# Twelve products of constants at each border between layers, in a whole network written as one kernel

## What is computed

```
x = x + nsa_mixer(rms_norm(x, ...), ...)                 # sparse attention, 16 heads
x = x + swiglu(rms_norm(x, ffn_norm[0]), ...)            # FFN 1
shared_k, shared_v = shared_mla_kv(x, ...)
x = x + mla_mixer(rms_norm(x, ...), shared_k, shared_v, ...)
x = x + swiglu(rms_norm(x, ffn_norm[1]), ...)            # FFN 2
# second block, two layers of
x = x + 0.5 * rmsnorm(ffn(rmsnorm(x, g_pre)), g_post)    # FFN 3, FFN 5
x = x + rmsnorm(mixer(rmsnorm(x, mix_pre)), mix_post)    # convolution, then differential attention
x = x + 0.5 * rmsnorm(ffn(rmsnorm(x, g_pre)), g_post)    # FFN 4, FFN 6
```

## Time and profile before

| | |
|---|---|
| median of 3 runs | 1904.44 us (1902.37 to 1904.89) |
| span of the profiled execution, first to last instruction | 1903.4 us |
| TensorE busy in it | 1733.7 us (91%) |
| VectorE, ScalarE, GpSimd busy | 1227.8, 815.2, 38.3 us |
| mean granted clock of TensorE | 0.959 of full speed |
| DMA | 285.93 MB, mean 150 GB/s |

### The profile page before, as it was taken

The page is one execution under the profiler, slowest core; times in us unless marked ns, Lnnn a source line. Parts: engine busy times, 40 slices in busy tenths (PEclk is TensorE's granted clock), DMA queues, the critical chain, the costliest instruction groups (busy, mean ns, idle before and its releaser), DMA issues.

```text
span 1903.4 us, 29255 instructions
## 1 busy us (share of the span) xinstructions
PE 1733.7 (91%) x11365; PEld 1593.9 (84%) x11365; DVE 1227.8 (65%) x1737; ACT 815.2 (43%) x1199; POOL 38.3 (2%) x23
## 2 busy tenths in 40 slices
PE   7879999997697999999989869999999989689997
PEld 7857799986577999899988769998899979579997
DVE  4778566666666666666668856665665654856665
ACT  4556443335444333533443054333443344743333
POOL 0000000000004000000000000000000000000000
PEclk9979999998799999999989989999899989889999
DMA  7510344453223455455444034545345445035444
GB/s 266 207 45 1 101 166 179 185 192 117 88 70 124 180 190 190 145 195 189 175 155 155 1 120 168 188 175 197 143 172 194 183 159 166 1 100 199 176 187 165
DMA packets 53291, 285.93 MB, mean 150 GB/s; under 512 B 5872, under 2 KB 6128, under 8 KB 30704
## 3 DMA queue, kind: packets, MB, share of 16 engines
q1 hardware_dynamic: 52224, 281.46, 41.0%
q0 software_dynamic: 1008, 3.67, 0.6%
HBM read 284.05 MB, written 1.05 MB: 150 GB/s over the span
## 4 chain that ended last, share of the span: by engine, by line
PE 79%; DVE 13%; ACT 5%; issue 2%; DMA 1%; SPq 0%; DVEq 0%; ACTq 0%
PE bank L812 18%; PE bank L814 17%; PE bank L813 17%; PE bank L955 9%; PE bank L923 3%; PE bank L925 3%; PE bank L927 3%; DVE proj L1684 3%; PE bank L826 2%; PE bank L1012 1%; PE bank L971 1%; ACT whi L428 1%; PE bank L992 1%; DVE wlo L1242 1%; DMA raw<-in_stream 1%
## 5 line engine op out<-in xcount | busy, mean ns | idle before, releaser
L812 PE MATMUL bank<-hthi,whi 128*128 128x256 f32 x2240 | 639.2, 285 | 3.3 <-DVE wlo L1242 1.8
L813 PE MATMUL bank<-htlo,whi 128*128 128x256 f32 x2240 | 636.1, 284 | 0.0
L814 PE MATMUL bank<-hthi,wlo 128*128 128x256 f32 x2240 | 636.1, 284 | 0.0
L1236 DVE TENSOR_TENSOR wlo<-raw,whi 128x2048 fp32r<-128x2048 f32 x175 | 401.2, 2293 | 112.9 <-ACT whi L428 112.8
L812 PEld LDWEIGHTS bank<-hthi,whi 128*128 128x128 f32 x2240 | 432.3, 193 | 10.4 <-DVE htlo L1296 2.5
L813 PEld LDWEIGHTS bank<-htlo,whi 128*128 128x128 f32 x2240 | 432.1, 193 | 4.6
L814 PEld LDWEIGHTS bank<-hthi,wlo 128*128 128x128 f32 x2240 | 431.7, 193 | 0.0
L428 ACT ACTIVATE whi<-raw 128x2048 fp32r<-128x2048 f32 x175 | 333.2, 1904 | 60.4 <-DMA raw<-in_stream 43.1
L498 ACT ACTIVATE tr<-tr 128x256 f32<-128x256 f32 x132 | 55.1, 417 | 630.2 <-DVE tr L1311 630.2
L1311 DVE TENSOR_TENSOR tr<-bank,rb 128x512 f32<-128x512 f32 x132 | 91.2, 691 | 232.0 <-PE bank L814 231.8
L1242 DVE TENSOR_TENSOR wlo<-raw,whi 128x1024 fp32r<-128x1024 f32 x174 | 212.3, 1220 | 27.0 <-ACT whi L436 26.5
(11 more groups left out here) (236 smaller groups left out, 1939.5 us busy)
## 6 DMA issues: line engine op xcount, KB each, us to landing
raw<-in_stream SPq DMA_DIRECT2D x176, 1024.0 KB, 5.4
raw<-in_stream SPq DMA_DIRECT2D x176, 512.0 KB, 3.5
wide<-in_wide POOLq DMA_DIRECT2D x7, 512.0 KB, 4.0
x<-in_x SPq DMA_DIRECT2D x1, 1024.0 KB, 5.3
out<-x SPq DMA_DIRECT2D x2, 512.0 KB, 2.8
wide<-in_const SPq DMA_DIRECT2D x1, 960.0 KB, 15.4
const<-in_const SPq DMA_DIRECT2D x1, 897.0 KB, 12.9
cols<-in_cols SPq DMA_DIRECT2D x1, 340.0 KB, 7.7
```

The lines of the kernel that those rows point to most:

```text
L812: nc.tensor.matmul(out, whi_, mhi, start=start, stop=False)
L813: nc.tensor.matmul(out, whi_, mlo, start=False, stop=False)
L814: return nc.tensor.matmul(out, wlo_, mhi, start=False, stop=stop)
L1236: V.tensor_tensor(wlo[:, s, 0:UA], raw[:, s, 0:UA], whi[:, s, 0:UA].bitcast(F32), ALU.subtract)\
```

## The change

A new helper `fill(cnt)` issues `cnt` products of `ident` (stationary) and 256 columns of the causal table (moving) into `gub[1]`, each with start and stop, read by no one. `operand_ahead` gets a parameter `spare`: so many of them ahead of `one(0)`, and as many between `one(0)` and `one(1)`. `x_operand` passes 6 everywhere but at `op_attn` and `op_bq`, so nine borders get twelve each, 108 in all. Ahead of the first projection behind the first attention a wait for the load of the constants is added.

```
+            def fill(cnt):
+                for _ in range(cnt):
+                    nc.tensor.matmul(gub[1][:, 0:T], ident, const[:, KO["causal"]:KO["causal"] + T], start=True, stop=True)
-            def operand_ahead(name, src, there):
+            def operand_ahead(name, src, there, spare=0):
...
+                fill(spare)
                 one(0)
+                fill(spare)
                 one(1)
                 return ready
...
-                return operand_ahead(name, lambda t, c: x[:, t, c * P:(c + 1) * P], there)
+                return operand_ahead(name, lambda t, c: x[:, t, c * P:(c + 1) * P], there,
+                                     0 if name in ("op_attn", "op_bq") else 6)
...
             attention("nsa")
+            pe.wait_ge(s_ldk, 16)
             pe.wait_ge(s_ol, 8)
```

## The result

| | before | after |
|---|---|---|
| median | 1904.66 us (1902.37 to 1908.05, 4 runs) | 1913.26 us (1911.70 to 1914.91, 4 runs) |
| span of the profiled execution | 1903.4 us | 1909.8 us (its time: 1911.7 us) |
| TensorE busy | 1733.7 us (91%) | 1766.7 us (93%) |
| mean granted clock | 0.959 | 0.972 |

A forecast was written before the change was run, and what follows sets the result against it. TensorE, busy 91% of the span, was taken as the bound, losing time where it waits or runs at lower clock. Short borders +12.0 and long borders -4.1 give +7.9 on 1904.44, so 1912.3 us; range 1906.0 to 1917.0.

The forecast's parts named there:

- The price of a product: Each added product is two records, 0.44 us of TensorE at full clock; six are 2.6 us, 5.5 at the lower clock.
- The rival of a fill worth one record: Six products cost 1.3 us: 1902.4, no change (chance 0.09), or 1899.1 with the clock held at long borders (0.04).
- the chain of rounds: At short borders round 1, ScalarE, VectorE, round 3, ScalarE, VectorE, chunk 6 follow in turn, so the fills' delay goes through.
- Short borders: op_f1, op_kv and op_f3, with little or no wait for x: the fills cost +3.7, +3.4 and +4.4 us.
- third rival: Unseen slack at the borders takes the short losses down by half: +1.9 us, 1906.3; chance 0.05.
- The cover at op_f2: The delay behind op_f2 lands in TensorE's wait behind GpSimd's work: +0.5 us, or +3.7 if the cover failed.
- Long borders with 4.2 us of wait: op_conv, op_f5, op_qkv: first fill free in the wait, clock stays at 1.00: -1.2, -1.2 and -2.7 us.
- second rival: The clock falls all the same, second fill costs 5.5 us at all five long borders: 1930; chance 0.06.
- Long borders with 5.5 us of wait: op_f4 and op_f6: 0.6 gained if the clock stays, up to 1.6 lost if it falls; +0.5 us each.
- The rest was taken as nothing: Constants' wait, DMAs, ScalarE's and VectorE's programs add nothing; 1.3 us each way for clock falls elsewhere.
- The range: 1906.0 to 1917.0 us, from clocks held (+5.5) to both late falls (+9.8), with allowances and the slack case.

The follow-up runs named there:

- run 9: The change with products of 128 columns instead of 256: 1906.23 us (10 runs, two groups) against 1903.33 before, ratio 1.0043.
- run 2: The change with its twelve products kept only at op_f1, op_kv, op_f2 and op_f3: 1916.58 us against 1903.56 before, ratio 1.0066.
- run 7: The change with twelve and twelve products at op_f2 instead of six and six: 1913.11 us in one run.
- run 3: The change with only the six products ahead of round 0, at all nine borders: 1909.96 us (5 runs, two groups), ratio 1.0076 to before.
- run 4: The change with only the six products between rounds 0 and 1, at all nine borders: 1913.46 us, ratio 1.0056 to before.
- run 1: The change with its twelve products kept only at op_conv, op_f4, op_f5, op_qkv and op_f6: 1902.87 us against 1903.56 before, ratio 0.9996.
- run 6: The change refilled at the five long borders alone: nine or twelve products ahead of round 0, three behind round 1: 1894.17 us against 1903.20 before, ratio 0.9955.
- run 10: Run 6 plus six products behind round 1 of op_bq: 1906.07 us (11 runs, two groups) against 1903.33 before, ratio 0.9991.
- run 8: Long borders alone, wait ahead of round 0 filled with 34 or 46 transposes of 128 columns instead of products: 1900.10 us in one run.

## Why the prediction was right

The forecast was 1912.3 us and +7.9; the medians are 1913.26 us and +8.6, the spans +6.4. By its own steps:

- **The price of a product**, 0.44 us from two records of 0.22: 2.58 us for six against 2.6. Run 9, at half the width, gave 1.34. The rival of a fill worth one record falls with the 216 records; its arithmetic for the short borders (1.1, 1.2 and 1.8 us at half the price) was met by run 9 with 1.05, 1.35 and 1.85. That a hypothetical price gives the right losses when it is made real shows that the chain of rounds was read rightly. Its total was not met, 1902.4 against 1906.2 (1905.2 in the lower group): the long borders gave 4.9 us in run 9 and not 6.1.
- **Short borders**, 3.7, 3.4 and 4.4: 3.56, 3.45 and 4.34, and unchanged in run 2, alone. There was no slack at any of them, so the third rival falls too.
- **The cover at op_f2**: 0.5 was kept for one operation of VectorE left over; -0.05 in the change, and run 7 hid twice the fill.
- **Long borders with 4.2 us of wait**, -1.2, -1.2 and -2.7: -1.16, -1.02 and -2.61. The clock stayed at 1.00 through them, against the second rival. Runs 3 and 4 show that it took both fills of six there.
- **Long borders with 5.5 us of wait**: the term that was mis-sized. The prediction took +0.5 for each, as the middle between a clock that holds (-0.6) and one that falls just ahead of x (+1.6). They are two cases and no middle: +1.14 where it fell (op_f4; both in run 1), -0.56 where it held (op_f6). The sum came out near by having one of each, and that was luck: in the traces of runs 1 and 7, with the same fills at these two borders, the clock fell at both, at +1.1 each, 1.6 us more for the two than in the trace of the change. The fall at op_f4 came 1.2 us after x, not ahead of it as the step put it, so it struck the fill and not the transposes of round 0.
- **The rest was taken as nothing**, with 1.3 us allowed each way. It was -0.7 in sum, but made of pieces up to 3.0 us with both signs, from where the clock falls in stretches that the change does not touch and, in FFN 5, from a late load in the trace of before. That they nearly cancel is luck of these two executions; the profiled execution of the change is also the fastest of its four, 1.6 us under their median, which is most of the difference between 6.4 on the spans and 8.6 on the medians.
- **The range** rests on two small slips. With all five clocks held the terms give 12.0 - 6.3 = +5.7, not +5.5, and with both late falls +10.1, not +9.8. The measured time lies well inside either way.

So the change loses at places where TensorE was not waiting (11.3 us) more than it gains where it was (4.2), and run 6 shows that the gain alone, with nothing paid between the rounds, is 9 us.

## What to carry to other kernels

Work that holds up a clock is free only in a wait, so size each filler to its own wait (leave a few tenths of a microsecond), put it there and nowhere between the links of a chain, and leave it out at borders that look alike in the code but have no wait in the trace. Look for the second gap: a filled first wait gave 3.7 us and the small gap behind it another 5.4, because the clock that had been saved was lost there at three of five borders. And check a change of a few microseconds by more than one profile, since a stretch far away may answer to the shifted clock with more than was gained.

## What the runs showed that was not expected

- **A clock that does not come back.** At half clock TensorE ran products for 30 us with no gap that the trace shows (18.20 of 18.20 and 11.60 of 11.60 us busy, run 9) and the clock did not rise; with the same products begun at full clock it stayed up at 12.07 busy of 12.90 us. Whether it is up when they begin decides 15 us, and small shifts decide that. For run 9 this is shown by its profile. For the upper groups of run 3 (17 us) and run 10 (15 us) it is inferred, since their profiled executions are of the lower groups: from the like distance, and from the mean granted clock, which is lower by about 0.010 in the upper group of each of the three (0.955 against 0.965 in run 3). As an estimate that is 38 us more at half clock in 1910; run 9's profile shows 34 more in the attention. Whether the products on 64 rows, plain float32 or something else keeps the clock down was not tried.
- **Transposes hold the clock** as products do (run 8), at 0.11 us each, through 3.9 and 5.2 us of wait, and in the kernel before sixteen of them brought it back.
- **More delay cost less.** Doubling the fill at op_f2 (run 7) made the kernel no later than before at that place, -0.87 us, since both the wait behind GpSimd and the fall of the clock behind that wait went away.
